# The first weight pair of a decoder layer taken by k tile, its first activations issued by ScalarE, and the rest of the activations in eight pieces

## The chip, the core and the metric

One core of a Trainium2 chip runs the kernel. The metric is the time of one execution on the device in microseconds (us), as the median of several runs.

## What is computed

The reference is one hybrid decoder layer for 256 tokens with a model width of 2048, in float32. The opening, which matters here, is the memory branch:

```python
def _memory_attention(q, mem, mem_norm_g, w_mem_kv, q_g, k_g):
    m = _rms_norm(mem, mem_norm_g)
    kv = m @ w_mem_kv
    ...
```

Here mem is 256 x 2048 and w_mem_kv is 2048 x 2048. Behind it come a combined input projection, causal differential attention, chunkwise retention, attention over the memory tokens, three gated branch projections, an output projection and a SwiGLU feed-forward part with a residual.

## The kernel before

**Arithmetic.** Each float32 matmul is made of three passes over float32r operands: high half by high half, high half by low weights, low activations by high weights. ScalarE makes the high half by a copy that rounds, VectorE the low half by subtracting the high half from the original.

**Weights.** They come in pairs of k tiles: a pair is 2 x 128 rows by 512 columns, 512 KB, in one of four ring slots of `raw`, `w_hi` and `w_lo` (RING = 4). SyncE issues the loads (`load`, L258). The first four go out at once; load g from the fifth on waits until the low half of pair g - 4 is made (`lo_done`, L261). ScalarE splits a pair (L449 for the first four, `high` at L412 behind them), VectorE makes its low half (L793, then `low` at L760), and TensorE multiplies it (`pair`, L1237): 2 k tiles x 2 token blocks x 3 passes = 12 matmuls of 128x512.

**Activations of the memory branch.** The host lays mem out transposed (`mem_t`, 2048 x 256). It is loaded into `memT`, which lies in `proj`, in five pieces of 2, 2, 4, 4 and 4 k tiles (`MEM_PIECES`, `mem_piece` at L276, the transfer at L273). ScalarE makes the high half of each k tile, scaled with the norm gain (`high_input`, L427, into `oT_hi`), VectorE the low half (`low_input`, L779, into `oT_lo`). The division by the root mean square comes later. `g_cols` holds the gains (24 KB, issued at L284).

**Order.** The queues are written out by hand. SyncE issues weights 0, gains, piece 0 (k tiles 0 and 1), piece 1 (2 and 3), weights 1, piece 2 (4 to 7), weights 2, weights 3, piece 3 (8 to 11), then weights 4 behind its wait, piece 4 (12 to 15), weights 5, weights 6, weights 7, the rows of mem (1 MB each before loads 8 and 11), and so on. ScalarE's program (L444 to L464) first splits weights 0, then converts k tiles 0 to 3; then for each s of 1 to 3 splits weights s and converts k tiles 2 + 2s and 3 + 2s, waiting for pieces 2 and 3 at s = 1 and s = 3; then, for s = 0 to 2 of the next loop, converts k tiles 10 + 2s and 11 + 2s ahead of the split of weights 4 + s. VectorE follows in the same order (L791 to L798). TensorE (L1269 to L1275) runs 24 transposes of the identity into an unused bank as soon as the identity is there, and then the 32 pairs of the memory projection; pair s of the first eight waits for its low weights and for the low half of k tiles up to 2s + 1. Pair s uses k tiles 2s and 2s + 1. TensorE, ScalarE and VectorE take their instructions in program order, and an engine that waits holds back all that is behind.

Of the kernel before, what the change touches and what calls it, by code (L numbers as in the profile page):

```python
# [26 lines left out]
F32 = mybir.dt.float32  # L27
# [6 lines left out]
P = 128  # L34
D = 2048
TB = 2
# [31 lines left out]
N0, S0W, S0T, N1, S1W, S1T, S2W, S2T, N2, S3W, S3T, N3, D0, D1, D2, D3 = range(PARTS)  # L68
MEM_PIECES = ((0, 2), (2, 4), (4, 8), (8, 12), (12, 16))
NEG = -1.0e30  # L70
# [13 lines left out]
def program(nc, x, mem, positions, w_in, da_q_norm_g, da_k_norm_g, da_lambda_q1, da_lambda_k1,  # L84
# [6 lines left out]
    with ExitStack() as ctx:  # L91
# [114 lines left out]
        mem_in, x_in = [sem(f"mem_in{i}") for i in range(TB)], [sem(f"x_in{i}") for i in range(TB)]  # L206
        memT_in = [sem(f"memT_in{i}") for i in range(len(MEM_PIECES))]
        xT_in = [sem(f"xT_in{i}") for i in range(4)]
# [48 lines left out]
        def _(sp):  # L257
# [18 lines left out]
            def mem_piece(n):  # L276
                transposed(memT, mem_t, *MEM_PIECES[n], memT_in[n])

# [3 lines left out]

            load(w_kv2, 0, 0, 0, 0)
            const(g_cols[:], norm_gains, gains_in)  # L284
            mem_piece(0)
            for g in range(1, 32):
                if g in (1, 2, 4, 5):
                    mem_piece((1, 2, 4, 5).index(g) + 1)
                if g in (8, 11):
                    rows(0, mem, (g - 8) // 3, mem_in)  # L290
                if g in (15, 19):
                    rows(D, x, (g - 15) // 4, x_in)
                if g in (21, 23, 24, 26):
                    n = (21, 23, 24, 26).index(g)
                    sp.wait_ge(row_sq, 2)
                    transposed(xT, x_t, 4 * n, 4 * n + 4, xT_in[n])
                load(w_kv2, 2 * P * (g % 8), (g // 8) * NCOL, g, g)
            for dst, src in ((g_da[:, 0], da_q_norm_g), (g_da[:, 1], da_k_norm_g), (g_mem[:, 0], mem_q_norm_g),
                             (g_mem[:, 1], mem_k_norm_g), (g_sub[:], da_subln_g), (g_ret[:], ret_norm_g),
# [105 lines left out]
        def _(act):  # L405
# [36 lines left out]


            act.wait_ge(zeroed, 4)  # L444
            act.activation(nmx[:, 0, 0:1], minus_half[:, 0:1], ACT.Copy)

            for s in range(RING):
                act.wait_ge(loaded[s], 16)
                act.activation(w_hi[:, s], raw[:, s], ACT.Copy).then_inc(hi_done, 1)  # L449
                if s == 0:  # L450
                    act.wait_ge(gains_in, 16)
                    act.wait_ge(memT_in[0], 16)
                    high_input(0, range(2), oT_hi, memT)
                for n in range(1, 4):
                    if MEM_PIECES[n][0] == 2 + 2 * s:
                        act.wait_ge(memT_in[n], 16)
                high_input(0, range(2 + 2 * s, 4 + 2 * s), oT_hi, memT)


            for s in range(32):  # L460
                if s < 3:
                    if s == 1:
                        act.wait_ge(memT_in[4], 16)
                    high_input(0, range(10 + 2 * s, 12 + 2 * s), oT_hi, memT)  # L464
# [286 lines left out]
        def _(v):  # L751
# [36 lines left out]
            for p in range(2):  # L788
                v.nop().then_inc(acc_free[p], 1)

            for s in range(RING):  # L791
                v.wait_ge(hi_done, s + 1)
                v.tensor_tensor(w_lo[:, s], raw[:, s], w_hi[:, s].bitcast(F32), ALU.subtract).then_inc(lo_done, 1)  # L793
                low_input(0, range(2 + 2 * s if s else 0, 4 + 2 * s), oT_lo, oT_hi, memT)

# [437 lines left out]
        def _(pe):  # L1233
# [38 lines left out]

            for s in range(32):
                chunk_pair(G_KV + s, s, oT_hi, oT_lo, 0, s % 8, 8, U_KV + s // 16, (s // 8) % 2,
                           2 * s + 2 if s < 8 else None)  # L1275
# [304 lines left out]
```

## Time and profile before

| | us |
|---|---|
| median of 3 runs | 1655.17 |
| lowest and highest | 1653.87, 1655.59 |
| the profiled execution, its own time | 1655.45 |
| its span, first to last instruction | 1653.6 |
| TensorE busy in it | 1642.5 (99%) |
| VectorE, ScalarE busy | 1102.4 (67%), 853.1 (52%) |

The profile is of one execution, taken by the hardware profiler. PE is TensorE (PEld its weight loads), DVE is VectorE, ACT is ScalarE, POOL is GpSimd, SP is SyncE. A row of a timeline gives the start in us, the busy time, the engine, the line of the kernel, the operation, and what it writes and reads; in brackets stands how long the engine had been idle before it, and what ended that. A granted clock of 1.00 means 2.4 GHz on TensorE, 0.50 means 1.2 GHz.

### The profile page before, as it was taken

The page shows a single profiled execution, that of the slowest core. Times are in us where ns is not written, and L with a number is a line of the kernel's source. Part 1 is how long each engine was busy: PE and PEld are TensorE (multiplying, and loading weights), DVE is VectorE, ACT ScalarE, POOL GpSimd, SP SyncE. Part 2 cuts the span into 40 slices and gives each one's busy share as a digit, 9 for nine tenths or more (in the row PEclk, how much of TensorE's full clock was granted, in tenths as well). Part 3 has the DMA queues.
Part 4 walks back from the last instruction along what each step waited for, and adds up shares of the span by engine and source line. Part 5 has one row for each costly group of instructions (what it writes and reads, how often), then busy time and mean ns, then how long its engine had stood idle before and what let it go on. Part 6 is the DMA issues. An engine that isn't in the chain of part 4 may idle for free.

```text
span 1653.6 us, 21258 instructions
## 1 busy us (share of the span) xinstructions
PE 1642.5 (99%) x7472; PEld 1359.9 (82%) x7472; DVE 1102.4 (67%) x1123; ACT 853.1 (52%) x903; POOL 79.7 (5%) x73
## 2 busy tenths in 40 slices
PE   9999999999999999999999999999999999999999
PEld 7888888888888888888888878888888888888887
DVE  5565454554577776655555578788887887787783
ACT  6654544444555544444444545555555555555552
POOL 0000000000011000000000000100100100100101
PEclk9999999999999999999999999999999999999999
DMA  9866656566555556666655666876877877867875
GB/s 333 276 209 190 178 153 189 170 195 193 179 154 165 164 165 184 190 223 191 192 176 189 188 205 197 233 248 207 250 234 216 248 226 218 247 228 221 243 229 153
DMA packets 177978, 340.98 MB, mean 206 GB/s; under 512 B 11792, under 2 KB 16400, under 8 KB 177168
## 3 DMA queue, kind: packets, MB, share of 16 engines
q1 hardware_dynamic: 167056, 319.45, 60.6%
q0 software_dynamic: 10880, 20.97, 7.1%
q8 instruction: 26, 0.43, 0.1%
q14 instruction: 16, 0.13, 0.0%
HBM read 317.31 MB, written 2.10 MB: 193 GB/s over the span
## 4 chain that ended last, share of the span: by engine, by line
PE 86%; issue 9%; DVE 2%; POOL 1%; DMA 1%; ACT 1%; SPq 0%; DVEq 0%; ACTq 0%; POOLq 0%
PE acc L1237 44%; PE at L1455 7%; PE at L1453 7%; PE at L1454 7%; PE acc L1453 6%; PE acc L1455 6%; PE acc L1454 6%; PE at L1259 2%; POOL rstd L385 1%; DMA raw<-in_w_mem_kv 1%; DVE w_lo L760 0%; PE at L1312 0%; PE at L1297 0%; ACT w_hi L412 0%; DMA raw<-in_w_in 0%
## 5 line engine op out<-in xcount | busy, mean ns | idle before, releaser
L760 DVE TENSOR_TENSOR w_lo<-raw,w_hi 128x1024 fp32r<-128x1024 f32 x332 | 403.1, 1224 | 352.2 <-ACT w_hi L412 350.3
L412 ACT ACTIVATE w_hi<-raw 128x1024 fp32r<-128x1024 f32 x332 | 351.6, 1061 | 427.6 <-PE acc L1237 406.7
L1237 PE MATMUL acc<-w_hi,hT_hi 128*128 128x512 f32 x896 | 354.0, 395 | 0.0
L1237 PE MATMUL acc<-w_hi,hT_lo 128*128 128x512 f32 x896 | 349.1, 390 | 0.0
L1237 PE MATMUL acc<-w_lo,hT_hi 128*128 128x512 f32 x896 | 348.9, 389 | 0.0
L1129 DVE TENSOR_TENSOR f_lo<-f_raw,f_hi 128x2048 fp32r<-128x2048 f32 x84 | 192.2, 2288 | 44.5 <-ACT f_hi L686 44.2
L686 ACT ACTIVATE f_hi<-f_raw 128x2048 fp32r<-128x2048 f32 x84 | 160.8, 1914 | 73.3 <-PE acc L1455 66.2
L1237 PEld LDWEIGHTS acc<-w_hi,hT_hi 128*128 128x128 f32 x896 | 168.2, 188 | 36.2 <-issue 1.3
L1237 PEld LDWEIGHTS acc<-w_hi,hT_lo 128*128 128x128 f32 x896 | 168.2, 188 | 35.6
L1237 PEld LDWEIGHTS acc<-w_lo,hT_hi 128*128 128x128 f32 x896 | 168.3, 188 | 33.8
L1237 PE MATMUL acc<-w_hi,oT_hi 128*128 128x512 f32 x448 | 176.2, 393 | 1.8 <-DVE oT_lo L779 1.3
L1237 PE MATMUL acc<-w_hi,oT_lo 128*128 128x512 f32 x448 | 174.5, 390 | 0.0
L1237 PE MATMUL acc<-w_lo,oT_hi 128*128 128x512 f32 x448 | 174.4, 389 | 0.0
L1453 PE MATMUL acc<-f_hi,hT_hi 128*128 128x512 f32 x400 | 157.0, 393 | 0.0
L1455 PE MATMUL acc<-f_hi,hT_lo 128*128 128x512 f32 x400 | 155.9, 390 | 0.0
L1454 PE MATMUL acc<-f_lo,hT_hi 128*128 128x512 f32 x400 | 155.9, 390 | 0.0
L1139 DVE TENSOR_TENSOR f_lo<-sum,f_hi 128x2048 fp32r<-128x2048 f32 x40 | 91.6, 2290 | 55.4 <-ACT f_hi L696 55.4
L1453 PE MATMUL at<-f_hi,aT_hi 128*128 128x512 f32 x320 | 124.6, 389 | 0.0
L1455 PE MATMUL at<-f_hi,aT_lo 128*128 128x512 f32 x320 | 124.6, 389 | 0.0
L1454 PE MATMUL at<-f_lo,aT_hi 128*128 128x512 f32 x320 | 124.5, 389 | 0.0
L696 ACT ACTIVATE f_hi<-sum 128x2048 fp32r<-128x2048 f32 x40 | 76.7, 1917 | 66.1 <-PE acc L1455 45.0
L1237 PEld LDWEIGHTS acc<-w_hi,oT_hi 128*128 128x128 f32 x448 | 84.1, 188 | 19.9 <-issue 1.6
(211 smaller groups left out, 1971.4 us busy)
## 6 DMA issues: line engine op xcount, KB each, us to landing
raw<-in_w_in SPq DMA_DIRECT2D x208, 512.0 KB, 3.8
f_raw<-in_w_ffn_down SPq DMA_DIRECT2D x88, 512.0 KB, 4.7
f_raw<-in_w_ffn_gate SPq DMA_DIRECT2D x80, 512.0 KB, 4.0
f_raw<-in_w_ffn_up SPq DMA_DIRECT2D x80, 512.0 KB, 4.8
proj<-down POOLq DMA_DIRECT2D x40, 512.0 KB, 7.3
raw<-in_w_mem_kv SPq DMA_DIRECT2D x32, 512.0 KB, 6.3
raw<-in_w_out SPq DMA_DIRECT2D x32, 512.0 KB, 4.5
raw<-in_w_o_mem SPq DMA_DIRECT2D x16, 512.0 KB, 5.6
```

The lines of the kernel that those rows point to most:

```text
L385: nc.gpsimd.tensor_tensor(rstd[:, 0:n], ms[:, 0:n], minus_half[:, 0:n], ALU.pow).then_inc(done, 1)
L412: act.activation(w_hi[:, s % RING], raw[:, s % RING], ACT.Copy).then_inc(hi_done, 1)
L686: act.activation(f_hi[p % SLOTS][:], f_raw[u % RAWS][:], ACT.Copy).then_inc(part_hi, 1)
L696: act.activation(f_hi[p % SLOTS][:], sums[i % 2][:], ACT.Copy).then_inc(part_hi, 1)
L760: v.tensor_tensor(w_lo[:, s % RING], raw[:, s % RING], w_hi[:, s % RING].bitcast(F32), ALU.subtract).then_inc(lo_done, 1)
L1129: v.tensor_tensor(f_lo[p % SLOTS][:], f_raw[u % RAWS][:], f_hi[p % SLOTS][:].bitcast(F32), ALU.subtract).then_inc(part_lo, 1)
L1139: v.tensor_tensor(f_lo[p % SLOTS][:], sums[i % 2][:], f_hi[p % SLOTS][:].bitcast(F32), ALU.subtract).then_inc(part_lo, 1)
L1237: e = pe.matmul(acc[p][:, t, :], a[:, k0 + k, tok], w[:, s % RING, k, :], start=first and k == 0 and n == 0, stop=last and k == 1 and n == 2)
L1259: return pe.transpose(out, src, ident[:])
L1453: pe.matmul(dst, hi, whi[:, b, :], start=first, stop=False)
L1454: pe.matmul(dst, hi, wlo[:, b, :], start=False, stop=False)
L1455: return pe.matmul(dst, lo, whi[:, b, :], start=False, stop=last)
```

## The change

The first weight pair is loaded as two transfers of one k tile each, with a semaphore of its own for the first (`tile_in`). ScalarE splits, and VectorE halves, each of the two tiles by itself, with the conversion of k tiles 0 and 1 in between; TensorE multiplies the pair in a function of its own (`first_pair`), k tile by k tile, pass by pass, with a wait ahead of each pass instead of one wait ahead of all twelve. The first two activation tiles and the gains are issued by ScalarE instead of SyncE. The activations come in eight pieces of two k tiles instead of five pieces. Piece g is issued behind weights g instead of ahead of them. ScalarE waits for piece s + 1 before it converts k tiles 2 + 2s and 3 + 2s, which stands between its splits of weights s and s + 1, and for piece s + 5 ahead of the split of weights 4 + s, for s from 0 to 2.

```diff
--- before.py
+++ after.py
@@ -66,7 +66,7 @@
 PARTS, UNITS, SLOTS, RAWS, NS = 16, 12, 4, 3, 4
 ALIGN = 8
 N0, S0W, S0T, N1, S1W, S1T, S2W, S2T, N2, S3W, S3T, N3, D0, D1, D2, D3 = range(PARTS)
-MEM_PIECES = ((0, 2), (2, 4), (4, 8), (8, 12), (12, 16))
+MEM_PIECES = 8
 NEG = -1.0e30
 FAR = 3.0e7
 TWO_PI = (6.28125, 0.0019350051879882812, 3.019916050173085e-07)
@@ -204,7 +204,8 @@
         pair_used = sem("pair_used")
         acc_free = [sem(f"acc_free{i}") for i in range(2)]
         mem_in, x_in = [sem(f"mem_in{i}") for i in range(TB)], [sem(f"x_in{i}") for i in range(TB)]
-        memT_in = [sem(f"memT_in{i}") for i in range(len(MEM_PIECES))]
+        memT_in = [sem(f"memT_in{i}") for i in range(MEM_PIECES)]
+        tile_in, tile_hi, tile_lo = sem("tile_in"), sem("tile_hi"), sem("tile_lo")
         xT_in = [sem(f"xT_in{i}") for i in range(4)]
         x_again = sem("x_again")
         const_in = sem("const_in")
@@ -274,18 +275,15 @@
                              src[k0 * P:k1 * P, :].rearrange("(k p) c -> p k c", p=P)).then_inc(done, 16)
 
             def mem_piece(n):
-                transposed(memT, mem_t, *MEM_PIECES[n], memT_in[n])
+                transposed(memT, mem_t, 2 * n, 2 * n + 2, memT_in[n])
 
             def rows(c0, src, t, done):
                 sp.dma_start(proj[:, t, c0:c0 + D], src[0, t * P:(t + 1) * P, :]).then_inc(done[t], 16)
 
 
-            load(w_kv2, 0, 0, 0, 0)
-            const(g_cols[:], norm_gains, gains_in)
-            mem_piece(0)
+            for k, done in enumerate((tile_in, loaded[0])):
+                sp.dma_start(raw[:, 0, k], w_kv2[k * P:(k + 1) * P, 0:NCOL]).then_inc(done, 16)
             for g in range(1, 32):
-                if g in (1, 2, 4, 5):
-                    mem_piece((1, 2, 4, 5).index(g) + 1)
                 if g in (8, 11):
                     rows(0, mem, (g - 8) // 3, mem_in)
                 if g in (15, 19):
@@ -295,6 +293,8 @@
                     sp.wait_ge(row_sq, 2)
                     transposed(xT, x_t, 4 * n, 4 * n + 4, xT_in[n])
                 load(w_kv2, 2 * P * (g % 8), (g // 8) * NCOL, g, g)
+                if g < MEM_PIECES:
+                    mem_piece(g)
             for dst, src in ((g_da[:, 0], da_q_norm_g), (g_da[:, 1], da_k_norm_g), (g_mem[:, 0], mem_q_norm_g),
                              (g_mem[:, 1], mem_k_norm_g), (g_sub[:], da_subln_g), (g_ret[:], ret_norm_g),
                              (lam_in[:, 0, 0], da_lambda_q1), (lam_in[:, 0, 1], da_lambda_q2),
@@ -441,26 +441,31 @@
                 e.then_inc(acc_free[p], 1)
 
 
+            act.dma_start(memT[:, 0, 0:2, :],
+                          mem_t[0:2 * P, :].rearrange("(k p) c -> p k c", p=P)).then_inc(memT_in[0], 16)
+            act.dma_start(g_cols[:], norm_gains).then_inc(gains_in, 16)
             act.wait_ge(zeroed, 4)
             act.activation(nmx[:, 0, 0:1], minus_half[:, 0:1], ACT.Copy)
 
+
+            act.wait_ge(tile_in, 16)
+            act.activation(w_hi[:, 0, 0], raw[:, 0, 0], ACT.Copy).then_inc(tile_hi, 1)
+            act.wait_ge(gains_in, 16)
+            act.wait_ge(memT_in[0], 16)
+            high_input(0, range(2), oT_hi, memT)
+            act.wait_ge(loaded[0], 16)
+            act.activation(w_hi[:, 0, 1], raw[:, 0, 1], ACT.Copy).then_inc(hi_done, 1)
             for s in range(RING):
-                act.wait_ge(loaded[s], 16)
-                act.activation(w_hi[:, s], raw[:, s], ACT.Copy).then_inc(hi_done, 1)
-                if s == 0:
-                    act.wait_ge(gains_in, 16)
-                    act.wait_ge(memT_in[0], 16)
-                    high_input(0, range(2), oT_hi, memT)
-                for n in range(1, 4):
-                    if MEM_PIECES[n][0] == 2 + 2 * s:
-                        act.wait_ge(memT_in[n], 16)
+                if s > 0:
+                    act.wait_ge(loaded[s], 16)
+                    act.activation(w_hi[:, s], raw[:, s], ACT.Copy).then_inc(hi_done, 1)
+                act.wait_ge(memT_in[s + 1], 16)
                 high_input(0, range(2 + 2 * s, 4 + 2 * s), oT_hi, memT)
 
 
             for s in range(32):
                 if s < 3:
-                    if s == 1:
-                        act.wait_ge(memT_in[4], 16)
+                    act.wait_ge(memT_in[s + 5], 16)
                     high_input(0, range(10 + 2 * s, 12 + 2 * s), oT_hi, memT)
                 if s in (9, 11):
                     row_squares(0, (s - 9) // 2, mem_in[(s - 9) // 2], 0)
@@ -788,10 +793,16 @@
             for p in range(2):
                 v.nop().then_inc(acc_free[p], 1)
 
+            v.wait_ge(tile_hi, 1)
+            v.tensor_tensor(w_lo[:, 0, 0], raw[:, 0, 0], w_hi[:, 0, 0].bitcast(F32), ALU.subtract).then_inc(tile_lo, 1)
+            low_input(0, range(2), oT_lo, oT_hi, memT)
+            v.wait_ge(hi_done, 1)
+            v.tensor_tensor(w_lo[:, 0, 1], raw[:, 0, 1], w_hi[:, 0, 1].bitcast(F32), ALU.subtract).then_inc(lo_done, 1)
             for s in range(RING):
-                v.wait_ge(hi_done, s + 1)
-                v.tensor_tensor(w_lo[:, s], raw[:, s], w_hi[:, s].bitcast(F32), ALU.subtract).then_inc(lo_done, 1)
-                low_input(0, range(2 + 2 * s if s else 0, 4 + 2 * s), oT_lo, oT_hi, memT)
+                if s > 0:
+                    v.wait_ge(hi_done, s + 1)
+                    v.tensor_tensor(w_lo[:, s], raw[:, s], w_hi[:, s].bitcast(F32), ALU.subtract).then_inc(lo_done, 1)
+                low_input(0, range(2 + 2 * s, 4 + 2 * s), oT_lo, oT_hi, memT)
 
             for s in range(32):
                 if s < 3:
@@ -1270,7 +1281,25 @@
             for n in range(24):
                 turn(at[:, 3, 0:P], ident[:])
 
-            for s in range(32):
+            def first_pair():
+
+                for k in range(2):
+                    for n, (a, w) in enumerate(((oT_hi, w_hi), (oT_hi, w_lo), (oT_lo, w_hi))):
+                        if n == 0:
+                            pe.wait_ge(tile_hi if k == 0 else hi_done, 1)
+                            pe.wait_ge(col_hi, k + 1)
+                        elif n == 1:
+                            pe.wait_ge(tile_lo if k == 0 else lo_done, 1)
+                        else:
+                            pe.wait_ge(col_lo, k + 1)
+                        for t in range(TB):
+                            e = pe.matmul(acc[0][:, t, :], a[:, k, t * P:(t + 1) * P], w[:, 0, k, :],
+                                          start=k == 0 and n == 0, stop=False)
+                e.then_inc(pair_used, 1)
+
+            pe.wait_ge(acc_free[0], 1)
+            first_pair()
+            for s in range(1, 32):
                 chunk_pair(G_KV + s, s, oT_hi, oT_lo, 0, s % 8, 8, U_KV + s // 16, (s // 8) % 2,
                            2 * s + 2 if s < 8 else None)
             pe.wait_ge(col_lo, 2 * KD)
```

## Rows read from the trace of the kernel before

**Rows 1.** TensorE's waits over the whole span: us in total, times, longest

```profile
PE at L1259 <- DVE proj L1084: 3.3, 1, 3.3
PE at L1259 <- POOL ident L369: 2.0, 1, 2.0
```

**Rows 2.** Timeline of TensorE, 0 to 16 us (start us, busy us, instruction)

```profile
2.03 5.38 PE L1259 MATMUL at<-ident 128*128 128x128 f32 x24 [2.03 <-POOL ident L369]
8.69 0.47 PE L1237 MATMUL acc<-w_hi,oT_hi 128*128 128x512 f32 x1 [1.28 <-DVE oT_lo L779]
...
12.12 0.50 PE L1237 MATMUL acc<-w_hi,oT_hi 128*128 128x512 f32 x1 [0.43 <-DVE w_lo L793]
...
15.27 0.50 PE L1237 MATMUL acc<-w_hi,oT_hi 128*128 128x512 f32 x1
```

**Rows 3.** Chain of waits, 0 to 100 us: start us, us, what

```profile
15.27 84.84 PE acc L1237 x373
```

**Rows 4.** Timeline of ScalarE, 0 to 24 us

```profile
0.75 1.28 ACT L445 ACT_TABLE_LOAD   x1 [0.75 <-PEq L1562]
...
5.44 1.06 ACT L449 ACTIVATE w_hi<-raw 128x1024 fp32r<-128x1024 f32 x1 [3.19 <-DMA raw<-in_w_mem_kv]
...
9.75 1.06 ACT L449 ACTIVATE w_hi<-raw 128x1024 fp32r<-128x1024 f32 x1 [1.51 <-DMA raw<-in_w_mem_kv]
11.54 0.91 ACT L427 ACTIVATE oT_hi<-proj,g_cols 128x256 fp32r<-128x256 f32 x2 [0.73 <-DMA proj<-in_mem_t]
12.89 1.06 ACT L449 ACTIVATE w_hi<-raw 128x1024 fp32r<-128x1024 f32 x1 [0.44 <-DMA raw<-in_w_mem_kv]
...
17.37 1.05 ACT L412 ACTIVATE w_hi<-raw 128x1024 fp32r<-128x1024 f32 x1
18.61 0.91 ACT L427 ACTIVATE oT_hi<-proj,g_cols 128x256 fp32r<-128x256 f32 x2 [0.20 <-DMA proj<-in_mem_t]
19.92 1.06 ACT L412 ACTIVATE w_hi<-raw 128x1024 fp32r<-128x1024 f32 x1 [0.40 <-DMA raw<-in_w_mem_kv]
...
23.50 1.06 ACT L412 ACTIVATE w_hi<-raw 128x1024 fp32r<-128x1024 f32 x1 [0.77 <-DMA raw<-in_w_mem_kv]
```

**Rows 5.** Stretches: busy PE, PEld, DVE, ACT, POOL; granted clock, DMA share, GB/s

```profile
0.00:5.44 5.44, 3.41 (x16) 3.41 (x17) 0.00 (x0) 1.49 (x3) 1.84 (x11) 1.00 0.57 150
5.44:9.75 4.31, 3.03 (x15) 2.48 (x14) 2.81 (x5) 2.76 (x6) 0.00 (x0) 1.00 1.00 306
9.75:12.89 3.14, 2.71 (x12) 1.94 (x11) 2.04 (x3) 1.97 (x3) 0.00 (x0) 1.00 1.06 397
12.89:18.61 5.72, 5.59 (x25) 4.27 (x24) 4.70 (x9) 5.47 (x9) 0.00 (x0) 1.00 1.07 369
```

**Rows 6.** Timeline of SyncE's queue: issues of transfers

```profile
1.25 0.46 SPq L269 DMA_DIRECT2D g_cols<-in_norm_gains  x1
...
12.09 5.44 SPq L262 DMA_DIRECT2D raw<-in_w_mem_kv  x3
...
19.89 4.68 SPq L262 DMA_DIRECT2D raw<-in_w_mem_kv  x3
```

**Rows 7.** Transfers issued from 1.7 to 2.3 us: KB each, us to landing

```profile
proj<-in_mem_t SPq DMA_DIRECT2D x2, 256.0 KB, 4.8
g_cols<-in_norm_gains SPq DMA_DIRECT2D x1, 24.0 KB, 4.3
```

**Rows 8.** Timeline of VectorE around 10.8 us

```profile
10.84 1.23 DVE L793 TENSOR_TENSOR w_lo<-raw,w_hi 128x1024 fp32r<-128x1024 f32 x1 [1.50 <-ACT w_hi L449]
```

**Rows 9.** Timeline of TensorE around the gap at 987 to 991 us

```profile
990.81 1.94 PE L1259 MATMUL at<-ident,proj 128*128 128x128 f32 x8 [3.33 <-DVE proj L1084]
...
993.40 0.63 PE L1455 MATMUL acc<-f_hi,hT_lo 128*128 128x512 f32 x1
```

**Rows 10.** Busy time by stretch behind that gap (PEclk is the granted clock)

```profile
991.00:992.00 1.00, 1.00 (x6) 1.00 (x6) 1.00 (x1) 0.00 (x0) 0.00 (x0) 0.50 0.94 297
...
993.00:994.00 1.00, 1.00 (x4) 0.81 (x3) 1.00 (x2) 1.00 (x2) 0.00 (x0) 0.50 0.81 303
```

## The prediction

> **What bounds the kernel now.** I read the page first, then the waits of TensorE, then its timeline at the start. TensorE waits in three places that matter: 2.0 us for the identity at the start, 1.3 us for the low half of the activations, 0.4 us for a low weight half, and once 3.3 us far behind [rows 1, 2]. The timeline shows the opening: 24 warm-up transposes from 2.03 to 7.41 us, pair 0 of the memory projection from 8.69, pair 1 from 12.12, pair 2 from 15.27 [rows 2]. From 15.27 on the chain of waits is one unbroken run of matmuls (373 in 84.84 us) [rows 3]. So the only time that this edit can reach lies before 15.27, and the measure of success is not when pair 0 starts but **when TensorE stops waiting for good**. A pair is 12 matmuls; 84.84 / 373 = 0.2275 us each, 2.72 us a pair, and 0.1 more after a stall. Pair 4 (the fifth) therefore starts at 15.27 + 0.1 + 2 x 2.72 = 20.8 now, pair 5 at 23.5, pair 6 at 26.3.
>
> What feeds these pairs is the transfers. ScalarE's timeline shows each landing as the moment at which it stops waiting [rows 4]. With the KiB that SyncE has issued up to and with that transfer: 512 at 5.44 (weights 0), 1560 at 9.75 (weights 1), 2072 at 11.54 (activation tiles 4 to 7), 2584 at 12.89 (weights 2), 4632 at 18.61 (tiles 12 to 15), 5144 at 19.92 (weights 5), 6168 at 23.50 (weights 7). It is a straight line of some 355 KiB per us from 9.75 on, with the 16 DMA engines busy throughout [rows 5]. A transfer lands by its place in that line.
>
> **Part 1, pair 0 by k tile, and ScalarE as issuer.** The first half tile is 256 KB instead of 512. The first activations (256 KB) and the gains (24 KB) go out from ScalarE; each issue costs it some 0.46 us (SyncE's price for the gains [rows 6]), in a time when it waits anyway until 5.44 [rows 4]: free. SyncE's later transfers are issued about 1 us sooner (two issues, 0.46 + 0.47), but the DMA engines are the limit by then, so I count this at nothing. ScalarE's issues are nowhere in this trace; bounds are 0.5 us earlier (the first activations go out at 0.8 instead of 1.76 and share the engines with the first half tile) and 0.3 later (should the 1.28 us table load [rows 4] run ahead of them). I take half tile 0 at 5.2, gains and first activations by 5.5 (a 256 KB piece took 4.8 us and the gains 4.3 [rows 7]). Half splits cost half of 1.06 and 1.23 [rows 4, 8], some 0.6 each; so the high half is there at 5.8, column 0 high at 6.3, low weights 6.5, column 0 low 7.1; tile 1 follows 0.9 to 1.1 later, and needs to be there only 6 x 0.23 = 1.4 later. All of it is ready before the transposes end at 7.4 [rows 2]. Pair 0 runs from 7.4 to 10.1 instead of 8.7 to 11.5. This **gains 1.3 us for pair 0**, and the one instruction more on each of ScalarE and VectorE costs nothing beside the waits of both.
>
> The Trainium skill (DMA: Bandwidth & Descriptors, Issuing engines are not separate DMA queues) says that transfers issued by several engines share the same 16 DMA engines and that only issue time is saved. No row here has a ScalarE transfer to show it; by that rule the line of landings stays where it is, and the sum below is unchanged.
>
> **Part 2, the activation pieces behind their weights, which is the part that decides.** ScalarE runs its program in order: it now waits for piece s+1 and converts its two columns before it splits weights s+1. Piece s+1 is issued behind weights s+1. So the split of a weight pair waits for a transfer that lands after the weights, plus two columns. The chain from that landing to TensorE: columns 0.91 [rows 4], split 9.75 to 10.84 = 1.09 [rows 4, 8], low half and start 10.84 to 12.12 = 1.28 [rows 8, 2]; together 3.28 us, against 2.37 today.
> - Pair 1: piece 1 is at 1560 KiB, as weights 1 are now: 9.75 + 3.28 = 13.0, against 12.12. The gain of pair 0 turns into an idle gap of 2.9 us.
> - Pair 2: piece 2 is at 2328 KiB, between two landings at 12.2: ready 15.5; TensorE comes at 13.0 + 2.83 = 15.9, against 15.27. The ring is then 0.6 behind.
> - Pair 3: piece 3 at 3096 KiB, 14.3: ready 17.6, wanted 18.6. Hidden.
> - Pair 4: in the next loop ScalarE waits for piece 5 ahead of weights 4. Piece 5 is at 4632 KiB, which landed at 18.61: ready 21.9, wanted 21.3. **TensorE stops 0.6 more.** Pair 4 starts at 21.9, against 20.8. Today its columns come from an earlier piece and its weights are split at 17.4.
> - Pair 5: piece 6 at 5400 KiB, 20.8: ready 24.1, wanted 24.7. Pair 6: piece 7 at 6168, 23.50: ready 26.8, wanted 27.4. Both hidden, the second by 0.6 us. Pair 8: its weights are issued when the low half of pair 4 is done, 21.8 instead of 19.9 [rows 6], and are wanted at 32.9; hidden.
>
> SyncE is held longer too: weights 5 and piece 5 wait for the low half of pair 1, done at 13.0 instead of 12.1 [rows 6], so piece 5 goes out at 13.5; with the 4.8 us of the first 256 KB pieces [rows 7], the shortest flights of any activation piece, it lands at 18.3 at best. Its bounds are 18.3 (pair 4 at 21.6) and, if the thinner queue lets the engines run dry for half a microsecond, 19.1 (pair 4 at 22.4).
>
> **Sum.** The end moves with pair 4: 21.9 - 20.8 = +1.1 us, bounds +0.8 and +1.6. The profiled execution took 1655.45 (span 1653.6 and 1.85 around it), so 1656.5 on its own basis; it lies 0.3 above the median of 1655.17, on which I put it: **1656.3 us**. Everything behind pair 6 is the same code on the same buffers. About 0.2% (3.3 us) is what a measurement of this kernel can tell from no change, so this counts as within it.
>
> **Rivals.**
> 1. *The clock falls in the new gap (slower side).* After the gap of 3.33 us at 990.81 the granted clock reads 0.50 from 991 to 994, which is 1.2 of 2.4 GHz, and matmuls take 0.63 instead of 0.39 [rows 9, 10]. After the idle 1.28 us at 8.69 nothing of this is seen: the clock reads 1.00 throughout [rows 2, 5]. My new gap is 2.9 us, nearer to the first. Three microseconds at half clock lose 1.5 us of work: pair 4 is wanted at 21.3 + 1.5 = 22.8 instead of ready at 21.9, so +2.0: 1657.2 us. It decides only when it costs more than the 0.6 us that pair 4 waits anyway. The Trainium skill (TensorE: Matmul & The Clock Gate, Why this matters for your kernels) warns in the same sense against idle gaps between bursts. The trace agrees at 990.81. Chance 0.2.
> 2. *Landings follow bytes moved, not place in the line (faster side).* Up to 9.75 the engines had moved 150 x 5.44 + 306 x 4.31 = 2135 KB [rows 5], 540 more than the 1597 that pair 1 needs; the rest belonged to transfers behind. If pieces of 256 KB land without that spread, piece 1 lands 540/387 = 1.4 us sooner at 8.35 and pair 1 starts at 11.6; weights 5 and piece 5 go out 1.4 sooner, piece 5 lands at 12.0 + 4.8 = 16.8, pair 4 starts at 20.1: -0.7, 1654.5 us. The limit is TensorE unbroken from 7.4: pair 4 at 18.4, -2.4, 1652.8. Against it: the line above held for pieces of either size. Chance 0.22.
> 3. *The head start is lost and nothing else changes:* the table load runs ahead of ScalarE's issues, pair 0 starts at 8.7 and later, and the gap shrinks. The end is still set by pieces 1 and 5: 1656.3. Inside the forecast.
>
> **How the numbers follow.** Forecast 0.52, clock 0.2, earlier landings 0.22, something not foreseen 0.06 (both signs). The three runs of before lie 1.7 us apart, so about 0.9 is added at each end: the range goes from 1653.8 (most of rival 2) to 1658.2 (rival 1 and 1). Beyond 3.3 us faster no case reaches, 0.02; beyond 3.3 us slower only the clock and a late piece 5 together, or an unforeseen delay, 0.05; within 0.93.
>
> **What the profile after would show.** Right: pair 0 near 7.4; ScalarE waiting for the activation transfer, not the weights, ahead of pairs 1 and 4; an idle TensorE of nearly 3 us ahead of pair 1 and a short one at pair 4; unbroken matmuls from 21 to 22. Rival 1: a granted clock of 0.5 around 13 to 16. Rival 2: pair 1 before 12.1 and no wait at pair 4. Wrong altogether: waits behind 30 us, or a difference away from the first 25.

## The result and the profile after

The changed kernel takes 1658.05 us (median of 15 runs, 1656.11 to 1660.42), the kernel before, run beside it, 1655.04 us (1653.87 to 1656.13). The ratio is 1.0017, with a 95% interval of 1.0010 to 1.0025: **3.0 us slower**. That is clear of zero and inside the 0.2% (3.3 us) that the forecast called "within". The profiled execution took 1659.21 us, of which 1657.1 are its span, 3.5 more than before. It lies 1.2 above the median, so the sum is held against the median.

TensorE's waits over the whole span (us in total, times, longest), in place of [rows 1]:

```profile
PE at L1270 <- DVE proj L1095: 3.3, 1, 3.3
PE acc L1296 <- ACT oT_hi L427: 2.1, 1, 2.1
PE at L1270 <- POOL ident L369: 2.0, 1, 2.0
PE acc L1248 <- DVE w_lo L765: 1.8, 1, 1.8
```

There is a new one, 1.8 us for a low weight half, and the wait ahead of pair 0 has grown from 1.28 to 2.1 us. TensorE's timeline, in place of [rows 2]:

```profile
2.03 4.62 PE L1270 MATMUL at<-ident 128*128 128x128 f32 x24 [2.03 <-POOL ident L369]
8.71 0.82 PE L1296 MATMUL acc<-w_hi,oT_hi 128*128 128x512 f32 x2 [2.06 <-ACT oT_hi L427]
...
11.03 1.05 PE L1296 MATMUL acc<-w_hi,oT_hi 128*128 128x512 f32 x2
...
13.13 0.49 PE L1248 MATMUL acc<-w_hi,oT_hi 128*128 128x512 f32 x1
...
23.34 0.50 PE L1248 MATMUL acc<-w_hi,oT_hi 128*128 128x512 f32 x1 [1.77 <-DVE w_lo L765]
```

Pair 0 starts at 8.71 us, no sooner than before (8.69). Its matmuls stand two to a row, and two take 1.05 us, at a granted clock of 0.50 (0.62 us in the run of the pair 0 part alone, at 1.00). Pair 1 follows at 13.13 with no idle time before it. Pair 4 starts at 23.34, behind the 1.8 us. In the kernel before it starts at 20.8, as the prediction worked out:

```profile
20.84 0.39 PE L1237 MATMUL acc<-w_hi,oT_hi 128*128 128x512 f32 x1
```

Why, ScalarE's timeline shows (in place of [rows 4]). The first two rows are its own issues of transfers:

```profile
0.75 0.47 ACTq L444 DMA_DIRECT2D proj<-in_mem_t  x1
1.25 0.48 ACTq L446 DMA_DIRECT2D g_cols<-in_norm_gains  x1
1.77 1.28 ACT L448 ACT_TABLE_LOAD   x1 [1.77 <-issue]
...
5.18 0.63 ACT L452 ACTIVATE w_hi<-raw 128x512 fp32r<-128x512 f32 x1 [1.91 <-DMA raw<-in_w_mem_kv]
8.06 0.91 ACT L427 ACTIVATE oT_hi<-proj,g_cols 128x256 fp32r<-128x256 f32 x2 [2.25 <-DMA g_cols<-in_norm_gains]
...
9.96 0.91 ACT L427 ACTIVATE oT_hi<-proj,g_cols 128x256 fp32r<-128x256 f32 x2 [0.47 <-DMA proj<-in_mem_t]
...
16.80 0.91 ACT L427 ACTIVATE oT_hi<-proj,g_cols 128x256 fp32r<-128x256 f32 x2 [0.87 <-DMA proj<-in_mem_t]
20.17 0.91 ACT L427 ACTIVATE oT_hi<-proj,g_cols 128x256 fp32r<-128x256 f32 x2 [2.46 <-DMA proj<-in_mem_t]
20.98 1.04 ACT L412 ACTIVATE w_hi<-raw 128x1024 fp32r<-128x1024 f32 x1
```

The first half tile is there at 5.18. Then ScalarE waits until 8.06, and for the **gains**. Further down it waits for activation pieces (the longer waits end at 9.96, 16.80 and 20.17), and at 20.17 piece 5 holds up the split of weights 4, which starts at 20.98 against 17.37 before. ScalarE's transfers, KB and us to landing, against 4.8 and 4.3 us in [rows 7]:

```profile
proj<-in_mem_t ACTq DMA_DIRECT2D x1, 256.0 KB, 5.4
g_cols<-in_norm_gains ACTq DMA_DIRECT2D x1, 24.0 KB, 6.8
```

SyncE's second half tile, issued at 1.20 us, is nearly as late as the gains, issued at 1.25:

```profile
raw<-in_w_mem_kv SPq DMA_DIRECT2D x1, 256.0 KB, 6.7
```

SyncE's queue, in place of [rows 6]. The first row is weights 4, the second weights 5 and the third piece 5:

```profile
10.24 0.37 SPq L263 DMA_DIRECT2D raw<-in_w_mem_kv  x1
...
13.10 0.37 SPq L263 DMA_DIRECT2D raw<-in_w_mem_kv  x1
13.51 0.47 SPq L274 DMA_DIRECT2D proj<-in_mem_t  x1
```

Weights 4 went out at 7.78 in the kernel before:

```profile
7.78 0.37 SPq L262 DMA_DIRECT2D raw<-in_w_mem_kv  x1
```

They wait for the low half of pair 0. Before, both tiles of weights 0 were split and halved ahead of the first activations. Now the second tile comes behind the conversion of k tiles 0 and 1, and that waits for the gains. The stretches that answer to [rows 5] (columns as there):

```profile
9.75:12.89 3.14, 3.14 (x9) 2.48 (x8) 2.39 (x4) 2.68 (x6) 0.00 (x0) 0.55 1.06 373
12.89:18.61 5.72, 5.72 (x26) 4.57 (x25) 5.08 (x9) 3.80 (x7) 0.00 (x0) 1.00 0.89 275
```

From 12.89 to 18.61 the transfers move 275 GB/s, not 369, and the DMA share is 0.89, not 1.07. That the engines run short of transfers, because the loads go out late, is a reading of these rows; the experiments come back to it. The chain of waits from there on, in place of [rows 3] (start us, us, what):

```profile
13.51 6.63 DMA proj<-in_mem_t
...
23.34 76.69 PE acc L1248 x337
```

So piece 5 issued at 13.51 sets the start of pair 4, and behind that all is matmuls. How far the opening moves the rest is told by the first square roots of the memory heads on GpSimd, some 320 us of unchanged work later; the first row is of the kernel before, the second of the changed one:

```profile
343.44 2.90 POOL L385 TENSOR_TENSOR rstd<-ms,minus_half 128x16 f32<-128x16 f32 x1 [51.62 <-DVE ms L786]
```

```profile
346.08 2.90 POOL L385 TENSOR_TENSOR rstd<-ms,minus_half 128x16 f32<-128x16 f32 x1 [51.62 <-DVE ms L791]
```

The shift is 2.64 us, 2.5 of it at pair 4. By 991 us it is 2.2 (990.81 and 993.04; no row here shows where the 0.4 is regained), and at the end 3.5. The 1.3 us between arise at or behind the gap ahead of the feed-forward part, which is 3.33 us long in both kernels. TensorE behind it in the changed kernel, in place of [rows 9, 10]:

```profile
993.04 1.94 PE L1270 MATMUL at<-ident,proj 128*128 128x128 f32 x8 [3.33 <-DVE proj L1095]
```

```profile
993.00:994.00 1.00, 0.96 (x5) 0.99 (x6) 1.00 (x1) 0.00 (x0) 0.00 (x0) 0.50 0.86 246
...
998.00:999.00 1.00, 1.00 (x3) 0.76 (x3) 1.00 (x1) 0.00 (x0) 0.00 (x0) 0.50 0.00 0
```

The granted clock stays at 0.50 for 6.9 us (992.2 to 999.0), twice as long as in the kernel before (3.4 us, 990.9 to 994.3). The code there is the same in both kernels. The last experiments take this gap out of the comparison.

### The profile page after: what moved, and what is told of

Same layout as the page of the kernel before. It is cut to its first block, busy times and chain, and to the rows that moved or that the text cites. A ratio compares the mean times of both kernels' runs of the same rounds, so it can differ in the third digit from the quotient of the medians.

```text
span 1657.1 us, 21265 instructions
## 1 busy us (share of the span) xinstructions
PE 1644.2 (99%) x7472; PEld 1361.2 (82%) x7472; DVE 1102.7 (67%) x1124; ACT 852.8 (51%) x904; POOL 80.7 (5%) x73
## 4 chain that ended last, share of the span: by engine, by line
PE 97%; DVE 1%; DMA 1%; ACT 0%; issue 0%; SPq 0%; ACTq 0%
PE acc L1248 53%; PE at L1484 7%; PE at L1482 7%; PE at L1483 7%; PE acc L1482 6%; PE acc L1484 6%; PE acc L1483 6%; PE at L1270 2%; DMA proj<-in_mem_t 1%; PE at L1341 0%; PE at L1326 0%; DVE w_lo L765 0%; PE at L1377 0%; ACT w_hi L412 0%; PE at L1375 0%
```

## The experiments

Theories at the start. **Order:** ScalarE takes piece s + 1 or s + 5 ahead of the weights that TensorE wants next, and these pieces are issued behind loads that wait. **Gains:** the gains land late on ScalarE's queue, with them the first low half, with it the load of weights 4, and the transfers run thin. **Clock:** what TensorE loses behind its new idle time. All medians stand beside the kernel before in the same series (1655.55 for e1 to e4, 1654.90 for e5 to e8, 1655.55 for e9 to e12). "Shift" is the move of the square roots above against 343.44, from one profile each.

| | weights 4 issued | pair 1 | pair 4, if it waits | shift | median less before |
|---|---|---|---|---|---|
| before | 7.78 | 12.12 | no wait | 0 | 0 |
| changed | 10.24 | 13.13 | 23.34 | +2.64 | +3.0 |
| e1, pair 0 part alone | 10.35 | 12.66 | no wait | +0.31 | +0.55 |
| e2, pieces part alone | 7.47 | 12.46 | 21.38 | +0.69 | +0.2 |
| e3, gains by SyncE | 8.73 | 11.81 | 21.75 | +1.22 | +0.9 |
| e4, pieces ahead | 10.26 | 13.15 | no wait | +0.68 | +0.6 |
| e5, 34 transposes | 10.09 | 12.98 | 23.49 | +4.43 | +3.6 |
| e6, weights first | 10.19 | 12.88 | no wait | +0.38 | +0.7 |
| e7, weights first, gains by SyncE | 8.84 | 11.23 | no wait | -1.32 | -0.5 |
| e8, gains issued first | 9.48 | 12.48 | 22.78 | +3.71 | one profile |

**e1, the pair 0 part alone.** From the changed kernel, the five pieces, their places and ScalarE's waits for them restored:

```diff
-MEM_PIECES = 8
+MEM_PIECES = ((0, 2), (2, 4), (4, 8), (8, 12), (12, 16))
...
             for g in range(1, 32):
+                if g in (1, 2, 4, 5):
+                    mem_piece((1, 2, 4, 5).index(g) + 1)
...
-                if g < MEM_PIECES:
-                    mem_piece(g)
```

> The pair 0 part alone: half tiles, ScalarE as issuer of the first activations and the gains, the five pieces in the old order. Order theory (what costs is that ScalarE waits for piece s+5 ahead of weights 4+s, and pieces come behind weights): pair 4 starts at 21.0 to 21.5 us without a wait for it, ratio 1.000 to 1.0005. Gains theory (what costs is that the gains land at 8.05 on ScalarE's queue, so that the first low half and with it the load of weights 4 come 2.5 us late and the queue of transfers runs thin): weights 4 issued near 10.2, pair 4 at 22.5 or later, ratio about 1.0015. Either way pair 0 near 8.7 and half clock behind it.

Measured: ratio 1.0007 (0.9998 to 1.0016). Weights 4 go out at 10.35, as late as in the changed kernel, yet nothing waits at pair 4. The rate over the stretch from 12.89 to 18.61, with the columns as above, is that of the kernel before (371 against 369 GB/s):

```profile
12.89:18.61 5.72, 5.72 (x26) 4.62 (x26) 4.97 (x10) 5.47 (x9) 0.00 (x0) 1.00 1.08 371
```

So late weights 4 alone do not starve the transfers, and the late gains alone do not make the loss. The half clock that was expected behind pair 0 was not seen in this profile.

**e2, the pieces part alone.** From the kernel before, eight pieces behind their weights and ScalarE's waits for them:

```diff
-                if g in (1, 2, 4, 5):
-                    mem_piece((1, 2, 4, 5).index(g) + 1)
...
                 load(w_kv2, 2 * P * (g % 8), (g // 8) * NCOL, g, g)
+                if g < MEM_PIECES:
+                    mem_piece(g)
```

> The pieces part alone: one load for pair 0, SyncE issues all, eight pieces behind their weights, ScalarE's waits as in the changed kernel. Order theory: pair 0 at 8.7, pair 1 at 13.0, pair 4 at 22 to 23, ratio 1.0007 to 1.0015. Gains theory: weights 4 issued at 7.8, pair 4 at 20.8 to 21.3, ratio 1.000 to 1.0003.

Measured: ratio 1.0006 (0.9997 to 1.0015). TensorE's timeline:

```profile
12.46 0.50 PE L1234 MATMUL acc<-w_hi,oT_hi 128*128 128x512 f32 x1 [1.08 <-DVE w_lo L790]
...
21.38 0.50 PE L1234 MATMUL acc<-w_hi,oT_hi 128*128 128x512 f32 x1 [0.42 <-DVE w_lo L757]
```

The mechanism of the prediction is there by itself: later pair 1, a wait at pair 4. By itself it costs little, 0.69 us of shift and 0.2 in the median. So neither part alone gives the loss: the shifts are 0.31 and 0.69, together 1.0, where the change has 2.64. **The parts work on each other.**

**e3, the gains back to SyncE.**

```diff
+            const(g_cols[:], norm_gains, gains_in)
             for g in range(1, 32):
...
-            act.dma_start(g_cols[:], norm_gains).then_inc(gains_in, 16)
```

> The changed kernel with the gains issued by SyncE behind the two half tiles. Gains land at 5.6 to 6.5 us instead of 8.05, pair 0 starts at 7.1 to 7.4. Order theory: pair 1 near 13, so the gap and the fall of the clock move behind pair 0, pair 4 at 22 or later, ratio 1.0007 to 1.0015. Gains theory: weights 4 issued below 8.5 us, pair 4 at 21 or earlier, ratio 0.9995 to 1.0003.

Measured: ratio 1.0008 (0.9999 to 1.0017). TensorE's timeline:

```profile
7.20 0.70 PE L1296 MATMUL acc<-w_hi,oT_hi 128*128 128x512 f32 x2 [0.67 <-ACT oT_hi L428]
...
11.81 0.50 PE L1248 MATMUL acc<-w_hi,oT_hi 128*128 128x512 f32 x1 [1.60 <-DVE w_lo L804]
...
21.75 0.50 PE L1248 MATMUL acc<-w_hi,oT_hi 128*128 128x512 f32 x1 [1.49 <-DVE w_lo L765]
```

With the gains landed at 6.5, pair 0 starts at 7.20: the head start of the prediction, and as it said, it ends in a gap ahead of pair 1 (1.60 us). Pair 4 is 1.6 us sooner than in the changed kernel but still waits 1.5. So each theory holds in part: without the late gains over half of the shift is gone, and a wait at pair 4 is left. More than the gains came sooner, though. The first activations took 4.5 us instead of 5.4 and the second half tile 5.1 instead of 6.7, and over the first 8 us the transfers ran at 232 GB/s instead of 201. Piece 1 ended ScalarE's wait at 8.64 instead of 9.96. So e3 tests the place of the gains with all that hangs on it, and not their landing alone.

**e4, each piece ahead of its weights.** `mem_piece(g)` moved from behind `load` to the head of the loop.

> The changed kernel with each of the eight pieces issued ahead of its weights instead of behind them. Order theory: pieces 4 to 7 no longer stand behind a load that waits for a low half, so piece 5 lands before 18.5 and pair 4 starts at 21.3 without a wait; ratio 1.000 to 1.0007 (the clock still falls behind 9 us). Gains theory: pair 4 still near 23, ratio about 1.0015.

Measured: ratio 1.0005 (0.9996 to 1.0015), and no wait of TensorE behind pair 0, though weights 4 go out at 10.26:

```profile
12.89:18.61 5.72, 5.72 (x26) 4.69 (x25) 5.33 (x10) 4.51 (x9) 0.00 (x0) 0.98 1.05 366
```

Piece 5 now goes out right behind weights 4, at 10.67 instead of 13.51, and the rate stays at 366 GB/s. This is what the order theory wanted, and with e1 it rules out that the late issue of weights 4 is enough by itself.

**e5, 34 transposes instead of 24.**

```diff
-            for n in range(24):
+            for n in range(34):
```

> The changed kernel with 34 warm-up transposes instead of 24, so that TensorE is busy until the first activations are ready near 8.7 us. Clock theory (the fall of the clock behind the idle 2.1 us is a part of the loss): granted clock 1.00 throughout the first 30 us, and pair 4 earlier than 23.3, ratio 1.000 to 1.001. Landing theory (pair 1 starts when its low weights are there, at 13.1, and pair 4 when piece 5 has landed, clock or not): clock 1.00 too, but pair 0 merely ends sooner, pair 1 at 13.0 to 13.2 and pair 4 at 23 to 23.5, ratio about 1.0015 as of the changed kernel.

Measured: ratio 1.0020 (1.0011 to 1.0029). TensorE's timeline, and a later stretch by windows:

```profile
12.98 0.50 PE L1248 MATMUL acc<-w_hi,oT_hi 128*128 128x512 f32 x1 [1.45 <-DVE w_lo L804]
...
23.49 0.50 PE L1248 MATMUL acc<-w_hi,oT_hi 128*128 128x512 f32 x1 [2.06 <-DVE w_lo L765]
```

```profile
24.00:25.00 1.00, 1.00 (x5) 0.77 (x5) 1.00 (x2) 0.19 (x1) 0.00 (x0) 0.76 1.07 402
25.00:26.00 1.00, 1.00 (x4) 0.81 (x3) 0.62 (x2) 0.71 (x2) 0.00 (x0) 0.50 0.83 309
```

The clock reads 1.00 from 8 to 24 us, and pair 1 and pair 4 start where they did (12.98, 23.49): the half clock during pair 0 cost the changed kernel nothing, as the landing theory had it. But here the clock falls behind the wait of 2.06 us ahead of pair 4, from about 24.5 to 27.9. Nothing hides that: the shift is 4.43, 1.8 more than the changed kernel's, of which the start of pair 4 explains 0.15 and the clock 1.6. e8's profile has the same fall behind a wait of 1.84 us. In the profile of the changed kernel the clock held behind 1.77 us. So this fall comes in some executions. That it is part of the wider spread of the changed kernel (4.3 us between lowest and highest, 2.3 before) is likely and not shown, as one execution of each kernel was profiled.

**e6, weights first.** ScalarE and VectorE take weights s and then the two tiles of the same pair; transfers as in the changed kernel. On ScalarE:

```diff
-                act.wait_ge(memT_in[s + 1], 16)
-                high_input(0, range(2 + 2 * s, 4 + 2 * s), oT_hi, memT)
+                act.wait_ge(memT_in[s], 16)
+                high_input(0, range(2 * s, 2 + 2 * s), oT_hi, memT)
...
-                    act.wait_ge(memT_in[s + 5], 16)
-                    high_input(0, range(10 + 2 * s, 12 + 2 * s), oT_hi, memT)
...
                 high(G_KV + s, s)
+                if s < 4:
+                    act.wait_ge(memT_in[s + 4], 16)
+                    high_input(0, range(8 + 2 * s, 10 + 2 * s), oT_hi, memT)
```

> The changed kernel with ScalarE and VectorE taking weights s first and then the two activation tiles of the same pair, so that nothing of pair s waits for the piece of pair s+1 or s+5-s; transfers and their order are as in the changed kernel, the gains still on ScalarE's queue. Order theory: pair 1 near 12 to 12.6 us, no wait of TensorE at pair 4, pair 4 at 20.5 to 21.5, ratio 0.9998 to 1.0006. If the thin queue alone did it (weights 4 issued at 10.2), pair 4 still waits and starts behind 22.

Measured: ratio 1.0003 (0.9994 to 1.0012). SyncE's issue of weights 4 first, then TensorE's waits:

```profile
10.19 0.37 SPq L263 DMA_DIRECT2D raw<-in_w_mem_kv  x1
```

```profile
PE at L1268 <- DVE proj L1093: 3.3, 1, 3.3
PE acc L1294 <- ACT oT_hi L427: 2.4, 1, 2.4
PE at L1268 <- POOL ident L369: 2.0, 1, 2.0
```

Weights 4 are as late as in the changed kernel, the pieces still stand behind the loads, and TensorE waits nowhere behind pair 0. Only ScalarE's and VectorE's programs differ. This settles the place: it is **the wait for a piece that the next pair does not need**, ahead of weights that it does. The order acts in two ways that this run does not part: the split of weights 4 no longer stands behind piece 5, and the low half of pair 1 is done sooner, so that weights 5 go out at 11.67 instead of 13.10.

**e7, both mended:** e3 and e6 together.

> Both mended: gains by SyncE behind the two half tiles, and weights s ahead of their own activation tiles on ScalarE and VectorE. Order and gains together: pair 0 at 7.2 us, pair 1 at 11.0 to 11.6, pair 4 at 19.3 to 20.3 without a wait behind pair 1, that is 0.5 to 1.5 us ahead of the kernel before: ratio 0.9990 to 0.9998. If a wait for transfers remains somewhere, pair 4 at 20.8 or later and ratio 1.000 or above.

Measured: median 1654.40 against 1654.90, ratio 0.9995 (0.9985 to 1.0004), the same within the interval. One of its eleven runs took 2779.69 us at a mean granted clock of 0.556; what lowered the clock is not known, and the median does not hang on that run. TensorE's timeline:

```profile
7.31 0.94 PE L1294 MATMUL acc<-w_hi,oT_hi 128*128 128x512 f32 x2
...
11.23 0.47 PE L1246 MATMUL acc<-w_hi,oT_hi 128*128 128x512 f32 x1 [0.68 <-DVE oT_lo L783]
```

Pair 0 from 7.31, pair 1 at 11.23, unbroken from there. The profile's shift is -1.32 us, as expected; the median gives 0.5 of it.

**e8, gains first on ScalarE's queue.** The two issues swapped.

> The changed kernel with ScalarE issuing the gains ahead of the first activations. If the gains are late because they stand behind 256 KB on ScalarE's own queue, they land at 4 to 5.5 us and ScalarE waits for the activations instead, pair 0 near 7.5. If a small-packet transfer on ScalarE's queue is slow wherever it stands (shared engines), it lands at 7 us or later and pair 0 stays near 8.5.

Measured, KB and us to landing (ScalarE's issues at 0.75 and 1.20):

```profile
g_cols<-in_norm_gains ACTq DMA_DIRECT2D x1, 24.0 KB, 4.4
```

```profile
proj<-in_mem_t ACTq DMA_DIRECT2D x1, 256.0 KB, 6.0
```

The gains land at 5.15 and the activations at 7.2. Neither expectation fits whole: the small transfer is as quick as on SyncE's queue when it is first, and whichever stands second on ScalarE's queue takes longer. Pair 0 starts at 7.95. Pair 4 still waits, until 22.78.

**e9, the mended order without the pair 0 part.** e2 with the order of e6.

> The pieces part alone as in e2 (SyncE issues everything, one load for pair 0), with weights s ahead of their own activation tiles on ScalarE and VectorE. Order theory: the wait ahead of weights 1 and 4 goes, pair 1 near 11.2 us, pair 4 at 19.6 to 20.2 without a wait of its own, ratio 0.9990 to 0.9999: as good as e7 without the k tile split and without ScalarE as issuer. If the head start of pair 0 (7.2 instead of 8.7) is worth something to the end, it stays 0.5 us or more behind e7 at pair 4.

Measured: 1655.47 against 1655.55, ratio 1.0000 (0.9991 to 1.0009); pair 1 at 11.88, not near 11.2, no wait behind it, shift -0.66. In the profiles e7 keeps a lead of 0.66 us over it, half of what e7 has over the kernel before. Whether the half tiles and the early pair 0 make this difference is not shown: single profiles of one kernel differ by more (e10), and medians 0.4 us apart don't tell the two from each other.

**e10 to e12, the far gap filled.** Fourteen transposes of the identity in the idle stretch ahead of the feed-forward part, in the kernel before (e10), the changed one (e11) and e7 (e12):

```diff
                 if first:
+                    pe.wait_ge(col_lo, 4 * KD)
+                    for n in range(14):
+                        turn(at[:, 3, 0:P], ident[:])
                     pe.wait_ge(acc_free[0], U_F0 + 2)
```

> The kernel before, with 14 more transposes of the identity into an unused part of PSUM in the idle 3.3 us ahead of the feed-forward part. Clock theory (the idle stretch at 987 to 991 us makes the clock fall for a time that differs from run to run, and this is most of the spread of all these kernels): granted clock 1.00 around 985 to 1000, ratio 0.9985 to 0.9995, lowest and highest of the runs less than 1.5 us apart. If the clock there costs nothing: ratio 1.000, spread as before (2.4 us).

> The changed kernel with the same 14 transposes. The difference to e10 is then the cost of the change at the opening alone: 2.5 us for the wait at pair 4, and up to 1.6 more where the clock falls behind that wait. So the median is 2.5 to 4.1 us above e10, and the runs still spread over more than 1.5 us. If the +3.0 us of the change came in part from the gap far behind, the difference is below 2.5.

> e7 (gains by SyncE, weights ahead of their own activation tiles) with the same 14 transposes. Pair 4 about 1.3 us sooner than in the kernel before and no fall of the clock: 1.0 to 1.5 us below e10, ratio to the kernel before 0.9978 to 0.9990, so that it beats both kernels. If e7's median of -0.5 was all there is, the ratio is as e10's less 0.0003.

| | median | lowest to highest | ratio to the kernel before | shift |
|---|---|---|---|---|
| e10, before, filled | 1653.10 | 1652.60 to 1654.10 | 0.9989 (0.9980 to 0.9998) | -1.04 |
| e11, changed, filled | 1656.33 | 1655.72 to 1658.85 | 1.0009 (1.0000 to 1.0018) | +1.98 |
| e12, e7, filled | 1652.95 | 1652.40 to 1653.37 | 0.9986 (0.9977 to 0.9995) | -1.40 |

TensorE's timeline at the gap in e10, the fourteen and then the eight of the kernel itself:

```profile
986.16 1.69 PE L1259 MATMUL at<-ident 128*128 128x128 f32 x14
989.64 1.06 PE L1259 MATMUL at<-ident,proj 128*128 128x128 f32 x8 [1.79 <-DVE proj L1084]
```

The fourteen took 1.69 us and not the 3.1 that the pace of the first 24 (5.38 us) would give, so 1.79 us stay idle, and still the clock reads 1.00 from 988 to 1003 in all three. The median falls by 2.45 us and the spread from 3.9 us (33 runs) to 1.5 (11 runs). Most of what differs from run to run in the kernel before is this one gap. Between e11 and e10 lie 3.2 us: the cost of the change with the far gap taken out, so within the intervals (about 1.5 us either way for each) the 3.0 us were made at the opening. e11 still spreads over 3.1 us. e12 is the fastest of all, ahead of both kernels, but of its 2.6 us the gap gives 2.45 and the mended opening some 0.15, within the spread. The 1.0 to 1.5 below e10 that were expected did not come; e7's small median was all there is. The kernel before with the gap filled (e10) also had a better opening in its profile than without (shift -1.04, no wait behind pair 0), which says how far an opening moves from one execution to the next. So does e11, with the opening of the changed kernel: piece 5 sets pair 4 off at 22.43 there, 0.9 us sooner than in the profile above. Shifts of 1 us and below are read with that in mind.

## Why the prediction was right, and where a term was off

**What bounds the kernel, and where the edit can reach.** Right. The loss is made before the matmuls become unbroken, and e10 and e11, 3.2 us apart, leave nothing of the 3.0 for the rest, within their intervals.

**Pair 0 by k tile.** Wrong in its timing. The text took "half tile 0 at 5.2, gains and first activations by 5.5". The half tile was right (5.18), the activations landed at 6.1 and the gains at 8.05. The step that failed is pricing the transfers at the start, now on two queues, by those of the kernel before on one (4.8 and 4.3 us; measured 5.4 and 6.8). SyncE's own second half tile was late as well (6.7). The rule cited there from the Trainium skill (DMA: Bandwidth & Descriptors, Issuing engines are not separate DMA queues), that only issue time is saved, fits the changed kernel: weights 1 went out at 1.67 instead of 2.74, and piece 1, at their old place in the line, landed no sooner (9.96 against 9.75). How late a single transfer lands on two queues, I could not draw from it. The split itself was priced right: with the gains back on SyncE (e3) pair 0 starts at 7.20, and the forecast said 7.4. That it would be lost to a gap ahead of pair 1 came true there too.

**Pieces behind their weights.** Right as a mechanism. Pair 1 was forecast for 13.0 and came at 13.13; pair 2 and 3 hidden, and they are; a wait at pair 4 for piece 5, and that is the wait; piece 5 issued at 13.5, and it was 13.51. The chain from a landing to TensorE, put at 3.28 us, took 3.17 (9.96 to 13.13, 20.17 to 23.34). e2, where the gains are not late, came at 12.46 and 21.38 against 13.0 and 21.9. That no idle time is seen ahead of pair 1 does not contradict the forecast of a gap there: pair 0 was late and at half clock, and filled it; where it ran at full clock (e5) 1.45 us stay idle. **The mis-sized term is the landing of piece 5**: 18.61 with bounds of 18.3 and 19.1; it landed at 20.16, and pair 4 started at 23.34 and not at 21.9. The text saw SyncE held for weights 5, by 0.9 us, and missed that weights 4 are held as well, by 2.5 us, because they wait for the low half of pair 0, whose second tile now waits for the gains. It gave a thinner queue half a microsecond at most.

Late weights 4 do not thin the queue alone: in e1 and e4 they are as late (10.35, 10.26), and the rate is 371 and 366 GB/s. The rate is low in all six profiles that have the pieces behind their loads and ScalarE's waits for them as in the changed kernel: 324 in e2, where weights 4 are early, 313 in e3, 303 in e8, and 275, 277 and 310 in the changed kernel, e5 and e11, where they are late. There 768 KB go out at 10.1 to 11.1 and nothing more until about 13. That the thin queue is what delays piece 5 is read from these rows; no run has tested it alone. What was tested is that it takes both: take the late gains away and 1.4 us of the shift go (e3), take the pieces' place away and 2.0 go (e4), take ScalarE's order away and 2.3 go (e6).

**Sum.** +1.1 forecast, +3.0 measured, 1658.05 us, inside the range (1653.8 to 1658.2) by 0.15 us. That it lies inside is luck. The sum's own bounds end at +1.6, and the upper end of the range was put there for rival 1 and for the spread of the runs, not for a piece 5 that lands at 20.16. Of the 1.9 missing, 1.4 is the late piece 5. The rest, 0.5, is not resolved. A fall of the clock behind the last wait in some executions would give such an amount, as it takes some 1.6 us where it comes (e5).

**The line of landings** was less straight than the text has it. From 1560 KiB at 9.75 to 6168 at 23.50 it is 335 KiB per us and not 355, and its stretches lie between 286 and 391. The landings of the pieces were read between neighbouring points, so the sum does not hang on the slope.

**Rival 1, the clock.** It does fall, already behind 2.06 us of idle time, but not where the rival put it: the fall behind the first gap costs nothing (e5), because pair 1 and pair 4 wait for transfers anyway. What costs is a fall behind the last wait, and the prediction had no term for that.

**Rival 2, earlier landings.** Not what happened in the changed kernel: piece 1 came at 9.96, 0.2 behind the line, piece 2 at 12.06, 0.15 ahead of it, and piece 5 1.5 behind. But the first half of the rival is seen in e3. There piece 1 came at 8.64 (the rival said 8.35) and pair 1 started at 11.81 (11.6). It did not reach the end, as piece 5 went out at 12.19 and came at 18.58 instead of 16.8. **Rival 3**, the table load ahead of ScalarE's issues: refuted, it runs behind them at 1.77. But its consequence, a lost head start, came from the gains.

## What to carry to other kernels

An engine that takes its program in order should wait for what the next consumer needs, and for nothing else. When transfers are moved, go through each wait on each engine once more: here a piece issued later turned a harmless early conversion into the wait that decides. And when a load waits for a first result, everything that this result waits for is on the load's path too; here a 24 KB table on a second queue held back half a megabyte of weights.

## What was not expected of the hardware

**With two queues in use, what stands second landed late on either.** 24 KB issued by ScalarE at 1.25 us behind 256 KB of its own took 6.8 us to land, against 4.3 on SyncE's queue in the kernel before; issued first they took 4.4 (e8), and then the 256 KB took 6.0. SyncE's half tiles, issued at 0.75 and 1.20, took 4.4 and 6.7, so the lateness is not ScalarE's alone. With the gains on SyncE's queue (e3) they took 3.8 and 5.1. Over the first 8 us the transfers ran at 199 to 209 GB/s in all six profiles with the gains second on ScalarE's queue, at 218 with them first (e8), and at 232 to 235 in the three with only the activations on it (e3, e7, e12). With all on SyncE's queue it was 198 to 211. Why so small a transfer costs so much, no run here shows.

**The clock record at the start.** The trace gives a granted clock of 1.00 from the first microsecond. But the transposes of the identity tell another thing. In order: the 24 at the start of the kernel before, the eight behind its far gap, where the record says 0.50, and the fourteen of e10 at 1.00 (ns min/median/max, first and last start):

```profile
L1259 PE MATMUL at<-ident x24: 421/421/473, 2.0 to 7.0; 128*128 128x128 f32 x24
```

```profile
L1259 PE MATMUL at<-ident,proj x8: 421/421/448, 990.8 to 992.3; 128*128 128x128 f32 x8
```

```profile
L1259 PE MATMUL at<-ident x14: 270/272/273, 986.2 to 987.6; 128*128 128x128 f32 x14
```

421 ns is what a transpose takes at 0.50, and 272 at 1.00. So the opening runs at half clock, whatever the record says, and a warm-up of 24 takes 5.38 us in one execution and 4.62 in another. The prediction read "1.00 throughout" around the 1.28 us gap as proof that a short gap is harmless, and that was weaker evidence than it looked: all 24 transposes ahead of that gap took 421 ns or more, at half clock, and the matmuls behind it 0.39 us, at full clock. The gap stood where the clock rose, and not behind a stretch at full clock.

**One gap, three lengths of the fall.** Behind the same 3.33 us of idle time the half clock lasted 3.4 us in the kernel before, 6.9 in the changed one and did not come in e2, e5, e7 and e8. Idle stretches of 1.79 us in e10 to e12 brought none, 1.84 us in e8 did; 1.80 us ahead of pair 0 did in e4 and did not in e11. So whether the clock falls behind idle stretches of 1.8 to 3.3 us differed from execution to execution here, and fourteen transposes in one of them were worth 2.45 us, nearly as much as the change under study cost.
